# Two eight-head softmax loops: scores run one head further ahead, a table set is loaded before the first loop, and the second loop's key squares go to GpSimd

## The reference

```python
q = rms_norm_2(q, g_qn_mla) * (MLA_QK ** -0.5)      # mla: 8 heads of 96
k = rms_norm_2(k, g_kn_mla)
o_mla = causal_attention_blocks(q, k, v)
...
qm = rms_norm_2(heads(q_b), g_qn_moba) * (MOBA_HEAD_DIM ** -0.5)   # moba: 8 heads of 64
km = rms_norm_2(heads(k_b), g_kn_moba)
o_moba = moba_attention(qm, km, heads(v_b))
...
def causal_attention_blocks(q, k, v):      # for blocks of 128 queries
    s = jnp.einsum('bhqd,bhkd->bhqk', q[:, :, lo:hi], k[:, :, :hi])
    p = jax.nn.softmax(jnp.where(mask, s, -jnp.inf), axis=-1)
    outs.append(jnp.einsum('bhqk,bhkd->bhqd', p, v[:, :, :hi]))
```

## Time and profile before

| | us |
|---|---|
| median of 3 runs | 928.17 |
| lowest and highest run | 927.97, 928.52 |
| span of the profiled execution, first to last instruction | 930.3 |
| TensorE busy in that span | 875.0 |
| VectorE busy | 576.0 |
| ScalarE busy | 440.6 |
| GpSimd busy | 106.9 |

### The profile page before, as it was taken

How to read it: one execution, slowest core, us unless ns; L and a number is a source line. 1 busy time by engine, 2 the same in 40 slices (tenths; PEclk the granted TensorE clock), 3 DMA queues, 4 the chain that set the end, 5 groups by cost and what they waited for, 6 DMA issues and landing times.

```text
span 930.3 us, 12088 instructions
## 1 busy us (share of the span) xinstructions
PE 875.0 (94%) x5003; PEld 723.1 (78%) x5003; DVE 576.0 (62%) x704; ACT 440.6 (47%) x581; POOL 106.9 (11%) x73
## 2 busy tenths in 40 slices
PE   2999999899999999899999999999679999999997
PEld 2888788787887887777778777887678878888886
DVE  3595375676244667857577777776685565555552
ACT  5444376656853555534534444543145454444441
POOL 1000000211000003205033332332000000000000
PEclk9999999999999999989999999999899999999999
DMA  9635285364001736404545556546766545555521
GB/s 350 223 108 190 104 294 181 104 239 148 7 26 67 286 114 225 137 1 134 181 161 180 197 200 212 195 154 212 211 222 217 198 143 191 192 192 188 181 91 45
DMA packets 66784, 155.87 MB, mean 168 GB/s; under 512 B 2937, under 2 KB 6618, under 8 KB 66474
## 3 DMA queue, kind: packets, MB, share of 16 engines
q1 hardware_dynamic: 63424, 145.37, 46.0%
q0 software_dynamic: 2224, 7.67, 2.5%
q10 hardware_dynamic: 1082, 2.07, 0.8%
HBM read 146.70 MB, written 7.34 MB: 166 GB/s over the span
## 4 chain that ended last, share of the span: by engine, by line
PE 75%; DVE 13%; ACT 4%; issue 3%; DMA 3%; POOL 1%; ACTq 0%; DVEq 0%
PE bank L635 20%; PE bank L637 19%; PE bank L636 19%; DVE wlo L1435 4%; ACT whi L1102 2%; PE bank L734 1%; PE bank L628 1%; DMA vrows<-in_vecs 1%; DMA ring<-in_w_in 1%; PE bank L894 1%; PE bank L987 1%; DVE wlo L1430 1%; DVE hT_lo L1418 1%; PE bank L777 1%; PE bank L852 1%
## 5 line engine op out<-in xcount | busy, mean ns | idle before, releaser
L1435 DVE TENSOR_TENSOR wlo<-ring,whi 128x2048 fp32r<-128x2048 f32 (+1 forms) x106 | 259.7, 2454 | 159.8 <-ACT whi L1102 159.7
L1102 ACT ACTIVATE whi<-ring 128x2048 fp32r<-128x2048 f32 (+1 forms) x106 | 202.2, 1909 | 228.7 <-PE bank L637 198.7
L635 PE MATMUL bank<-whi,hT_hi 128*128 128x512 f32 (+1 forms) x736 | 290.5, 395 | 7.3 <-DVE hT_lo L1418 4.0
L636 PE MATMUL bank<-wlo,hT_hi 128*128 128x512 f32 (+1 forms) x736 | 286.7, 389 | 0.0
L637 PE MATMUL bank<-whi,hT_lo 128*128 128x512 f32 (+1 forms) x736 | 286.6, 389 | 0.0
L635 PEld LDWEIGHTS bank<-whi,hT_hi 128*128 128x128 f32 x736 | 138.5, 188 | 36.4 <-issue 3.8
L637 PEld LDWEIGHTS bank<-whi,hT_lo 128*128 128x128 f32 x736 | 138.6, 188 | 28.6
L636 PEld LDWEIGHTS bank<-wlo,hT_hi 128*128 128x128 f32 x736 | 138.7, 188 | 27.2 <-issue 0.2
L635 PE MATMUL bank<-whi,hidT_hi 128*128 128x512 f32 x256 | 100.6, 393 | 1.1 <-DVE hidT_lo L1929 1.1
L637 PE MATMUL bank<-whi,hidT_lo 128*128 128x512 f32 x256 | 99.7, 390 | 0.0
L636 PE MATMUL bank<-wlo,hidT_hi 128*128 128x512 f32 x256 | 99.7, 389 | 0.0
(11 more groups left out here) (271 smaller groups left out, 955.6 us busy)
## 6 DMA issues: line engine op xcount, KB each, us to landing
ring<-in_w_ff SPq DMA_DIRECT2D x64, 1024.0 KB, 5.3
ring<-in_a_w_in SPq DMA_DIRECT2D x8, 1024.0 KB, 8.4
ring<-in_ple_gate_w SPq DMA_DIRECT2D x8, 1024.0 KB, 5.1
ring<-in_w_kv SPq DMA_DIRECT2D x8, 1024.0 KB, 7.0
ring<-in_b_w_in SPq DMA_DIRECT2D x8, 1024.0 KB, 4.9
ring<-in_w_in SPq DMA_DIRECT2D x6, 1024.0 KB, 5.5
ring<-in_w_glu SPq DMA_DIRECT2D x6, 1024.0 KB, 6.4
ring<-in_a_w_out SPq DMA_DIRECT2D x4, 1024.0 KB, 5.3
```

The costliest lines, as they stand in the source:

```text
L635: pe.matmul(bank_cols, high[:, at[0], at[1]], w_high, start=first, stop=False)
L636: pe.matmul(bank_cols, high[:, at[0], at[1]], w_low, start=False, stop=False)
L1102: act.activation(whi[at], raw_rows(g), ACT.Copy).then_inc(high_made, 1)
L1435: dve.tensor_tensor(wlo[at], raw_rows(g), whi[at], ALU.subtract).then_inc(low_made, 1)
```

## The change

Four edits. `AHEAD = 3` replaces the constants of the two loops: T of head i-3 stands in step i (before i-2), the value products of head i-4 (before i-3), and a loop has twelve steps (before eleven). The ACT program names the table set "natural_log_exp_and_others" right after the second half fill that belongs to `wk`. The square of the `kmoba` rows is taken from DVE and given to GpSimd, between its third and fourth L2038. And the rest of `row_means("kmoba")` moves from step 2 to step 5 of the first loop, `row_scale("kmoba")` from step 5 to step 7.

```diff
+AHEAD = 3
 ...
-        for i in range(MH + 3):
+        for i in range(MH + AHEAD + 1):
             if i < MH:
                 u.add(("scores", kind, i), "a", bank=i % 4)
-            if 2 <= i < MH + 2:
-                u.add(("probsT", kind, i - 2), "v", bank=4 + i % 2)
+            if AHEAD <= i < MH + AHEAD:
+                u.add(("probsT", kind, i - AHEAD), "v", bank=4 + (i - AHEAD) % 2)
 ...
@@ scalar
                 if name == "wk":
                     refill(name, 1)
+                    act.preload_act_table_set("natural_log_exp_and_others")
@@ tensor
-                    if 2 <= i < MH + 2:
-                        n = i - 2
+                    if AHEAD <= i < MH + AHEAD:
+                        n = i - AHEAD
 ...
-                    if i >= 3:
-                        n = i - 3
+                    if i > AHEAD:
+                        n = i - AHEAD - 1
@@ vector
             def row_means(name):
                 buf, n, width = rows_of(name)
+                sq = squares[:, 0:16 * width].rearrange("p (n c) -> p n c", n=16)
+                link(dve.tensor_tensor(sq, buf, buf, ALU.mult))
+                square_means(name)
+
+            def square_means(name):
+                buf, n, width = rows_of(name)
                 headnorms[0] += 1
                 sq = squares[:, 0:16 * width].rearrange("p (n c) -> p n c", n=16)
-                link(dve.tensor_tensor(sq, buf, buf, ALU.mult))
                 link(dve.tensor_reduce(ssh[:, n], sq, AX_X, ALU.add))
 ...
-                    if kind == "mla" and i == 2:
-                        emptied(("wk", 0, 1))
-                        row_means("kmoba")
                     if kind == "mla" and i == 5:
+                        dve.wait_ge(squared, 1)
+                        square_means("kmoba")
+                    if kind == "mla" and i == 7:
                         row_scale("kmoba", 7)
@@ gpsimd
             for k, n in enumerate((slice(0, 16), slice(0, 16), slice(16, 32), slice(16, 32))):
+                if k == 3:
+                    pool.wait_ge(act_emptied, u.emptied(("wk", 0, 1)))
+                    pool.tensor_tensor(squares[:, 0:1024], work[:, 5120:6144], work[:, 5120:6144], ALU.mult)\
+                        .then_inc(squared, 1)
                 pool.wait_ge(headms_ready, 4 + k)
```

More of the change, by code:

```diff
@@ L214, in plan @@
             turned(u, name + kind, 4 if kind == "mla" else 2)
-        for i in range(MH + 3):
+        for i in range(MH + AHEAD + 1):
             if i < MH:
                 u.add(("scores", kind, i), "a", bank=i % 4)
-            if 2 <= i < MH + 2:
-                u.add(("probsT", kind, i - 2), "v", bank=4 + i % 2)
-            if i >= 3 and (i - 3) % 4 == 3:
-                u.add(("soft_out", kind, (i - 3) // 4), "v", bank=6 + (i - 3) // 4)
+            if AHEAD <= i < MH + AHEAD:
+                u.add(("probsT", kind, i - AHEAD), "v", bank=4 + (i - AHEAD) % 2)
+            if i > AHEAD and (i - AHEAD - 1) % 4 == 3:
+                u.add(("soft_out", kind, (i - AHEAD - 1) // 4), "v", bank=6 + (i - AHEAD - 1) // 4)
     turned_in_two(u, "o2")
@@ L410, in program @@
          regrouped, waves_turned, waves_ready, fades_ready, gelu_ready,
-         act_step, dve_step, pool_step, out_stored) = (
+         act_step, dve_step, pool_step, squared, out_stored) = (
             sem(n) for n in (
@@ L419, in program @@
                 "zeros_stored", "x_chunked", "rows_ready", "skips_scaled", "states_ready", "regrouped", "waves_turned", "waves_ready", "fades_ready",
-                "gelu_ready", "act_step", "dve_step", "pool_step", "out_stored"))
+                "gelu_ready", "act_step", "dve_step", "pool_step", "squared", "out_stored"))
         toep_landed, val_landed = ([sem(f"{n}_landed{b}") for b in range(2)] for n in ("toep", "val"))
@@ L1887, in _ @@
                             .then_inc(max_ready, 1)
-                    if 2 <= i < MH + 2:
-                        b = filled(("probsT", kind, i - 2))
-                        dve.tensor_copy(probsT[:, (i - 2) % 3, :], b[:, 0:384]).then_inc(dve_emptied, 1)
-                    if kind == "mla" and i == 2:
-                        emptied(("wk", 0, 1))
-                        row_means("kmoba")
+                    if AHEAD <= i < MH + AHEAD:
+                        b = filled(("probsT", kind, i - AHEAD))
+                        dve.tensor_copy(probsT[:, (i - AHEAD) % 3, :], b[:, 0:384]).then_inc(dve_emptied, 1)
                     if kind == "mla" and i == 5:
+                        dve.wait_ge(squared, 1)
+                        square_means("kmoba")
+                    if kind == "mla" and i == 7:
                         row_scale("kmoba", 7)
-                    if i >= 3 and (i - 3) % 4 == 3:
-                        k = (i - 3) // 4
+                    if i > AHEAD and (i - AHEAD - 1) % 4 == 3:
+                        k = (i - AHEAD - 1) // 4
                         b = filled(("soft_out", kind, k))
```

## The result

The change makes the kernel slower. Over 20 runs it takes 935.79 us (932.76 to 947.80); the kernel before, run 20 times beside it, 930.09 (927.10 to 948.25). The ratio is 1.0072, 95% interval 1.0049 to 1.0095. Forecast were 926.4 us, in a range of 923.2 to 930.2.

The account below looks back on a forecast made before the run. TensorE, busy 875.0 of 930.3 us, was taken as the bound. First loop 5.8 us shorter, less 2.3 for the square and 1.7 for one half-clock drop: 1.8 us gain from 928.17, so 926.4, range 923.2 to 930.2.

Parts of the forecast that it names:

- The table load: Moved into ScalarE's 3.00 us gap before 372.96: its 1.28 us fit there and cost nothing.
- One more head ahead: First loop: four scores ahead of the first T remove waits of 1.6 and 1.5 us; 5.1 more if clock holds.
- The tail: End of the first loop: TensorE waits 2.5 us for head 5's copy, late behind power, scaling and division.
- The square: Ahead of the first loop: GpSimd's square holds up VectorE's scaling, so the loop starts 2.3 us later.
- The second loop: Second loop: no wait at its start to remove, no scaling at its end; change 0, within 0.3 us.
- 5.1 more if the clock holds: First loop: half of the 10.2 us at half clock (392.0 to 402.2) counted as loss to win back.
- 5.8 and 3.5: First loop 16.8 us instead of 22.6, a gain of 5.8; less 2.3 for the square, 3.5 at full clock.
- as unchanged: The 2.1 us between the traced span (930.3) and the median (928.17) were assumed to stay the same.
- L: Microseconds at half clock between 380 and 410; forecast 3.4, one short drop, costing 1.7 us of the gain.
- the third rival: Slower: idle time ahead of first loop brings 10.2 us at half clock, its end another 3.4; 931.5 us, chance 0.12.

Follow-up runs that it names:

- run 20: Not a label, part of "run 20 times": the kernel before, unchanged, executed 20 times beside the changed kernel: 930.09 us (927.10 to 948.25).
- The part alone: Only the table load moved ahead, in the kernel before: 930.65 us, ratio 0.9977 (0.9946 to 1.0008).
- The run with the square moved: Changed kernel with GpSimd's square behind the scores of head 0, means and scaling one step earlier (4 and 6): 937.65 us, ratio 1.0018.
- before again: The kernel before, unchanged, profiled once more with the granted clock of every execution: 929.67 us, ratio 0.9986; 928.53 is its profiled execution.
- the second lot: The changed kernel, unaltered, run again on another chip beside the kernel before: 936.26 us, ratio 1.0060 (1.0026 to 1.0094).
- the 1.15 us left: Changed kernel, square behind head 0's scores, means and scaling one step earlier, only the idle time ahead of moba's first scores filled: 928.62 us, ratio 0.9973.

## Why the prediction was wrong

**The table load** was right: 1.28 us at 370.13, within the gap of the earlier trace rows. Of the Trainium skill's 2.66 us (ScalarE: Activation LUTs, What ACT_TABLE_LOAD costs) only the load shows, here and before; no drain is to be seen. The part alone is 0.9977 with 1 in its interval, so whether its wait of 1.44 us gave anything to the whole is open.

**One more head ahead** was right on the path: the first T waits for nothing, and no wait of the middle is left.

**The tail** was right in kind and near in size: 2.0 us of idle time instead of 2.5, by the chain that was named, power, scaling, division, copy.

**The square** was right in kind, its size a little high: VectorE's scaling was held by 1.7 us, not 2.3, TensorE's idle time was 2.13 instead of 2.6, first scores at 384.08 instead of 384.4. The run with the square moved shows the exclusion from both sides (1.75 and 1.89 us apart, 3.44 and 2.92 together). The Trainium skill's rule (SBUF — State Buffer, terms, shared port pair) agrees with the trace.

**The second loop** was to change by nothing, within 0.3. At full clock it takes 20.9 us instead of 20.5 (from its transposes to the next, all idle times filled: 400.81 to 421.67 and 400.45 to 420.95), so that term was missed by a little. The larger fault is that its clock was left out: in the profiles of four variants it is where the long half clock falls.

**The failed step is the sum's "5.1 more if the clock holds".** The 5.1 stands inside its 5.8 and 3.5. It counted the half clock of the earlier trace rows as a loss that every execution of the kernel before pays, and took the gain off a median, 928.17, whose executions, judging by their times, don't pay it: before again, at 928.53 us, has its first loop at full clock in 18.3 us. (Even where it is paid it is nearer 4.4, 22.6 less 18.3.) The warning stood in the rows: the span was 2.1 us above the median, when a span ought to lie below the time that holds it (1.8 below, in every profile since), so the profiled execution was some 4 us slower than the median. I took the 2.1 "as unchanged". Without the 5.1, the prediction's own sum at full clock reads 3.5 - 5.1 = -1.6: 1.6 us slower, not 3.5 faster. The runs with the loops' idle times filled measure that sum nearly free of the clock: changed 928.69, before 928.90. In their timelines the first loop takes 17.1 and 18.2 us (predicted 16.8 for the changed one), its scores start 1.5 us later, and the second loop takes 0.4 us longer: 0.7 us on the path instead of 1.6, a draw within 0.2%. The lines of the first scores and of the transposes for the second loop, changed and then before:

```profile
383.75 0.46 PE L859 MATMUL bank<-work 96*128 96x128 f32 x2 [0.19 <-DVE work L1420]
...
400.81 1.92 PE L629 MATMUL bank<-cst,work 128*128 128x128 f32 x16
```

```profile
382.24 0.46 PE L854 MATMUL bank<-work 96*128 96x128 f32 x2 [0.65 <-DVE work L1419]
...
400.45 1.92 PE L628 MATMUL bank<-cst,work 128*128 128x128 f32 x16
```

**The second error was L.** The forecast took one drop of 3.4 us. It was two of 6.8, 13.6 in all, exactly the length in the third rival, which had a chance of 0.12 and a price of 931.5; with the 5.1 not there to be won back, its time is 928.17 + 1.6 + 13.6/2 = 936.6, and 935.8 was measured. That this comes so near is partly luck, since the 1.6 measured 0.7 and the clock outside the loops differs too; the part in the loops, 21.6 against 17.1 us for the first loop and 3.62 against 1.92 for the transposes behind it, is 6.2 us. In hindsight the third rival deserved more than 0.12: two idle times of over 2 us replace two of 1.4, and of the changed kernel's 32 executions none had a mean clock of 0.989, against 17 of 35 of before beside the second lot. That the loss comes with these idle times is shown, by filling them: 936.3 us, and 929.5 with the two filled, 928.7 with the one ahead of the second loop too, for the same waits. What is not settled: why an idle time of 2.02 us once passed without loss and one of 0.92 us was followed by 31 us at half clock, and what sets the lengths, which run from 3.4 to 41 us. The runs give only odds: with all idle times from 0.9 us up, in the first loop and ahead of either loop, filled or removed, none of 36 executions was above 938, with the 1.15 us left none of 13 (the profiled one had 6.8 us at half clock behind it), with only some filled up to 8 of 12. The 1.02 us behind the second loop stayed idle in all of them.

## What to carry to other kernels

Ask first which execution the trace is: set its own time, or its span, and its mean granted clock against the list of runs, and never take off a median what only a slower execution pays. An edit that trades short waits for fewer but longer ones in a TensorE-bound stretch can be neutral on the path and still lose, here 6 to 7 us for two idle times of 2 us; so weigh the clock behind each new idle time, not only its length. Where an idle time can't be removed, a microsecond of useless transposes in it can be worth several, but fill all of them around a dense stretch and time a dozen executions: filling only some had a worse median and more executions above 938 us than filling none in two kernels here (942.2 against 936.3, 935.9 against 930.4), though their ratios don't tell the two apart.

## What the runs showed of the hardware that was not expected

- A stretch at half clock can hold for 30.7 to 41.0 us with TensorE busy for 97% of it. Being busy does not bring the clock back at once. It began 1.3 us after an idle time of 2.04 us had ended, and 2.4 us after one of 0.92.
- The clock can fall before an idle time is over: once at 396.1, in a wait of 2.28 us that ended at 396.68.
- The same kernel on the same chip, 35 times, shows mean clocks from 0.962 to 0.994 and times from 927.3 to 953.3 us, with no change to it.
- A product of 1024 elements with two inputs on GpSimd takes 1.89 us with no two-input operation of VectorE beside it and 2.92 with one, which in turn takes 3.44 instead of 1.75: one holds the other up, and 1.03 and 1.69 us are lost.
